# State-space loop: the adds on GpSimd set into VectorE's PSUM reads, two wide rotation passes on VectorE, output weights scaled by ScalarE

## What is computed

```
bbr = fr[..., None] * br - fi[..., None] * bi
bbi = fr[..., None] * bi + fi[..., None] * br
bu_r = jnp.einsum('blgc,gpc->blgp', uf, bbr)
bu_i = jnp.einsum('blgc,gpc->blgp', uf, bbi)
_, _, xr, xi = lax.associative_scan(_complex_affine_combine, (a_r, a_i, bu_r, bu_i), axis=1)
y = (jnp.einsum('blgp,gcp->blgc', xr, c_re) - jnp.einsum('blgp,gcp->blgc', xi, c_im)
     + d_skip * uf)
y = jax.nn.gelu(y.reshape(bsz, seq, SSM_WIDTH), approximate=False)
```

## Time and profile before

| | |
|---|---|
| median of 3 runs | 5059.5 us (5055.14 to 5059.69) |
| the profiled execution's own time | 5057.54 us |
| its span, first to last instruction | 5055.7 us |
| the loop's block, 256 to 430 us of the span | 174 us, 3.4% of the span |
| busy in that block | VectorE 160.9, TensorE 111.8, GpSimd 94.9, ScalarE 1.3 us |
| mean granted TensorE clock, whole span / in that block | 0.963 / 0.81 |

### The profile page before, as it was taken

One profiled execution on the slowest core, in us unless ns is written; L12 is line 12 of the kernel. 1 busy time (PEld: TensorE's weight loads), 2 busy tenths in 40 slices (PEclk: granted clock), 3 DMA queues, 4 the chain that ended last, 5 costly groups with the idle time before them and its releaser, 6 DMA issues. The chain is left out here.

```text
span 5055.7 us, 51526 instructions
## 1 busy us (share of the span) xinstructions
PE 4678.1 (93%) x19788; PEld 3543.7 (70%) x19788; DVE 2261.2 (45%) x4552; ACT 1444.6 (29%) x2163; POOL 1938.2 (38%) x884
## 2 busy tenths in 40 slices
PE   7667889999999999999999988899999997787999
PEld 6224757888888788888788745668878874355787
DVE  8697346983333233333440253454234136654440
ACT  3302322334444211111322234332222232233321
POOL 3054414446666444444444400334444431012443
PEclk9788989999999999999999989999999999998999
DMA  3011313445545656555222200212222221011222
GB/s 113 25 29 46 111 34 102 132 137 178 175 163 179 200 187 191 184 188 181 88 96 96 96 23 14 84 63 94 93 92 96 95 86 40 17 53 54 90 96 84
DMA packets 213172, 519.23 MB, mean 103 GB/s; under 512 B 16960, under 2 KB 82752, under 8 KB 210112
## 3 DMA queue, kind: packets, MB, share of 16 engines
q1 hardware_dynamic: 128448, 448.82, 27.0%
q10 hardware_dynamic: 84480, 67.12, 4.2%
HBM read 446.66 MB, written 69.21 MB: 102 GB/s over the span
## 5 line engine op out<-in xcount | busy, mean ns | idle before, releaser
L187 POOL TENSOR_TENSOR ring_rounded<-ring,highs_rounded 128x1024 fp32r<-128x1024 f32 x687 | 1683.7, 2452 | 2767.2 <-ACT highs_rounded L181 2767.2
L395 PE MATMUL bank<-arena_rounded,ring_rounded 128*128 128x512 f32 (+1 forms) x4488 | 1790.9, 399 | 99.6 <-DVE hT_rounded L413 41.4
L397 PE MATMUL bank<-arena_rounded,highs_rounded 128*128 128x512 f32 (+1 forms) x4488 | 1776.9, 396 | 0.0
L181 ACT ACTIVATE highs_rounded<-ring 128x1024 fp32r<-128x1024 f32 x687 | 727.9, 1061 | 2107.3 <-PE bank L397 1605.5
L396 PE MATMUL bank<-hT_rounded,highs_rounded 128*128 128x512 f32 x3128 | 1228.5, 393 | 0.0
L395 PEld LDWEIGHTS bank<-arena_rounded,ring_rounded 128*128 128x128 f32 x4488 | 854.0, 190 | 293.4 <-issue 86.1
L397 PEld LDWEIGHTS bank<-arena_rounded,highs_rounded 128*128 128x128 f32 x4488 | 852.6, 190 | 205.1
L396 PE MATMUL bank<-arena_rounded,highs_rounded 128*128 128x512 f32 (+1 forms) x2112 | 821.5, 389 | 0.0
L396 PEld LDWEIGHTS bank<-hT_rounded,highs_rounded 128*128 128x128 f32 x3128 | 593.3, 190 | 141.4
L396 PEld LDWEIGHTS bank<-arena_rounded,highs_rounded 128*128 128x128 f32 x2112 | 402.1, 190 | 86.9
L1248 DVE TENSOR_TENSOR arena<-qT,arena 128x512 f32<-128x512 f32 x64 | 150.6, 2354 | 372.2 <-ACT qT L1213 371.6
(11 more groups left out here) (325 smaller groups left out, 4684.9 us busy)
## 6 DMA issues: line engine op xcount, KB each, us to landing
ring<-pages_in SPq DMA_DIRECT2D x687, 512.0 KB, 3.4
act_table<-arena SPq DMA_DIRECT2D x128, 256.0 KB, 4.0
gate_table<-qT SPq DMA_DIRECT2D x16, 2048.0 KB, 7.3
arena<-act_table ACTq DMA_DIRECT2D x128, 256.0 KB, 4.0
arena<-gate_table ACTq DMA_DIRECT2D x32, 1024.0 KB, 8.4
arena<-ssm_in SPq DMA_DIRECT2D x16, 256.0 KB, 2.6
arena<-mem_in SPq DMA_DIRECT2D x3, 1024.0 KB, 4.8
xT<-x_in SPq DMA_DIRECT2D x8, 256.0 KB, 6.4
```

The lines of the kernel that those rows point to most:

```text
L181: nc.scalar.activation(f32r(page_high(p)), slot(p), ACT.Copy).then_inc(masked_pages.sem, 1)
L187: nc.gpsimd.tensor_tensor(f32r(slot(p)), slot(p), part_of(page_high(p)), ALU.subtract).then_inc(split_pages.sem, 1)
L395: low_last = nc.tensor.matmul(out, f32r(w_low), f32r(x_high), start=start, stop=False)
L397: return low_last, nc.tensor.matmul(out, f32r(w_high), f32r(x_high), start=False, stop=stop)
```

## The change

All of it is in `ssm`. For each tile:

- The fourth product of the turn carries a factor -1 (br * -1 * s), so that GpSimd's two instructions are both adds. `shifted` is signalled twice, after the second and after the fourth product. The first add waits for the first signal. The second add of tile t also waits for `weighed`, until VectorE is through with scan(t-1).
- The four products that turn the result forward are two instructions of 128x1024 on VectorE: both scanned halves, which now lie side by side, times cs into `by_cos`, and then times sn in place. GpSimd has no products any more.
- The output weights are made by ScalarE: four scaled copies of 128x128 (`scaled_c`), then one add of 128x256 on VectorE ahead of the scans, then a negated copy by ScalarE. They have three blocks for each tile in place of two.
- TensorE's matmuls are the same in number and shape; outputs(t) waits for `paired` and for the second `weighed`. SyncE's transfer for tile t waits for `made` and `scored` of tile t-4 and no longer for `mixed`.

The diff, with unchanged lines between left out:

```diff
     bct = [arena[:, 14592 + 512 * b:15104 + 512 * b].rearrange("p (m s) -> p m s", m=4) for b in range(depth + 1)]
-    cf = [arena[:, 16640 + 256 * b:16896 + 256 * b].rearrange("p (m s) -> p m s", m=2) for b in range(depth)]
+    cf = [arena[:, 16640 + 384 * b:17024 + 384 * b].rearrange("p (m s) -> p m s", m=3) for b in range(depth)]
+    scaled_c = arena[:, 17792:18304].rearrange("p (m s) -> p m s", m=4)
     tmp = [qT[:, 8 + j, :] for j in range(8)]
-    def part(t, j):
-        i = 4 * (t % depth) + j
-        return arena[:, 10496 + 512 * i:11008 + 512 * i] if i < 8 else hT[:, i - 4, :]
+    def halves(t, j):
+        if t % depth < 2:
+            at = 10496 + 2048 * (t % depth) + 1024 * j
+            return arena[:, at:at + 1024].rearrange("p (h n) -> p h n", h=2)
+        return hT[:, 4 + 2 * j:6 + 2 * j, :]
...
-                    sp.wait_ge(mixed.sem, mixed.at(t - depth))
+                    sp.wait_ge(made.sem, made.at(t - depth))
+                    sp.wait_ge(scored.sem, scored.at(t - depth))
                 sp.dma_start(bct[t % (depth + 1)], ssm_dram[t]).then_inc(drawn.sem, 16)
...
-                    pe.wait_ge(shifted.sem, shifted.at(t - 1))
+                    pe.wait_ge(shifted.sem, shifted.at(2 * (t - 1)))
                 for half in range(2):
...
-                pe.wait_ge(weighed.sem, weighed.at(t + 1))
-                pe.wait_ge(copied.sem, copied.at(t + 1))
-                for at, (c, j) in enumerate(((0, 0), (0, 2), (1, 1), (1, 3))):
-                    last = nc.tensor.matmul(bank[4 + t // 4][:], cf[t % depth][:, c, :], part(t, j),
+                pe.wait_ge(paired.sem, paired.at(t + 1))
+                pe.wait_ge(weighed.sem, weighed.at(2 * t + 2))
+                by_cos, by_sin = halves(t, 0), halves(t, 1)
+                for at, (c, moving) in enumerate(((0, by_cos[:, 0, :]), (2, by_sin[:, 1, :]),
+                                                  (1, by_sin[:, 0, :]), (1, by_cos[:, 1, :]))):
+                    last = nc.tensor.matmul(bank[4 + t // 4][:], cf[t % depth][:, c, :], moving,
                                             start=(t % 4 == 0 and at == 0), stop=(t % 4 == 3 and at == 3))
...
         def _(pool):
-            for t in range(n + 1):
-                if t < n:
-                    pool.wait_ge(shifted.sem, shifted.at(t + 1))
-                    nc.gpsimd.tensor_tensor(part(t, 0), part(t, 0), part(t, 1), ALU.add)
-                    nc.gpsimd.tensor_tensor(part(t, 2), part(t, 2), part(t, 3),
-                                            ALU.subtract).then_inc(summed.sem, 1)
-                if t >= 1:
-                    pool.wait_ge(exped.sem, exped.at(t))
-                    nc.gpsimd.tensor_tensor(part(t - 1, 0), part(t - 1, 1), cs[:, t - 1, :], ALU.mult)
-                    nc.gpsimd.tensor_tensor(part(t - 1, 1), part(t - 1, 1), sn(t - 1),
-                                            ALU.mult).then_inc(copied.sem, 1)
+            for t in range(n):
+                for h in range(2):
+                    pool.wait_ge(shifted.sem, shifted.at(2 * t + h + 1))
+                    if h == 1 and t >= 1:
+                        pool.wait_ge(weighed.sem, weighed.at(2 * t))
+                    nc.gpsimd.tensor_tensor(halves(t, 0)[:, h, :], halves(t, 0)[:, h, :], halves(t, 1)[:, h, :],
+                                            ALU.add).then_inc(summed.sem, 1)
...
                 br, bi = bank[2 * (t % 2)][:], bank[2 * (t % 2) + 1][:]
+                by_cos, by_sin = halves(t, 0), halves(t, 1)
                 if t >= depth:
...
                 dve.wait_ge(scored.sem, scored.at(t + 1))
-                nc.vector.tensor_tensor(part(t, 0), br, c, ALU.mult)
-                nc.vector.tensor_tensor(part(t, 1), bi, s, ALU.mult)
-                nc.vector.tensor_tensor(part(t, 2), bi, c, ALU.mult)
-                nc.vector.tensor_tensor(part(t, 3), br, s, ALU.mult).then_inc(shifted.sem, 1)
-                cr, ci = bct[t % (depth + 1)][:, 2, :], bct[t % (depth + 1)][:, 3, :]
-                cr2, ci2 = cf[t % depth][:, 0, :], cf[t % depth][:, 1, :]
-                dve.wait_ge(drawn.sem, drawn.at(16 * (t + 1)))
-                nc.vector.tensor_scalar(cr2, cr, fr[:, t:t + 1], None, ALU.mult)
-                link(nc.vector.tensor_scalar(ci2, cr, nfi[:, t:t + 1], None, ALU.mult))
-                nc.vector.scalar_tensor_tensor(out=cr2, in0=ci, scalar=nfi[:, t:t + 1], in1=cr2,
-                                               op0=ALU.mult, op1=ALU.add)
-                nc.vector.scalar_tensor_tensor(out=ci2, in0=ci, scalar=nfr[:, t:t + 1], in1=ci2,
-                                               op0=ALU.mult, op1=ALU.add)
+                nc.vector.tensor_tensor(by_cos[:, 0, :], br, c, ALU.mult)
+                nc.vector.tensor_tensor(by_sin[:, 0, :], bi, s, ALU.mult).then_inc(shifted.sem, 1)
+                nc.vector.tensor_tensor(by_cos[:, 1, :], bi, c, ALU.mult)
+                nc.vector.scalar_tensor_tensor(out=by_sin[:, 1, :], in0=br, scalar=-1.0, in1=s, op0=ALU.mult,
+                                               op1=ALU.mult).then_inc(shifted.sem, 1)
...
                 r = mag[:, t:t + 1].broadcast_to([P, SEQ])
-                dve.wait_ge(summed.sem, summed.at(t + 1))
-                nc.vector.tensor_tensor_scan(part(t, 1), r, part(t, 0), 0.0, ALU.mult, ALU.add)
-                nc.vector.tensor_tensor_scan(part(t, 3), r, part(t, 2), 0.0, ALU.mult,
+                by_cos, by_sin = halves(t, 0), halves(t, 1)
+                dve.wait_ge(copied.sem, copied.at(t + 1))
+                nc.vector.tensor_tensor(cf[t % depth][:, 0:2, :], scaled_c[:, 0:2, :], scaled_c[:, 2:4, :],
+                                        ALU.add).then_inc(made.sem, 1)
+                dve.wait_ge(summed.sem, summed.at(2 * t + 2))
+                nc.vector.tensor_tensor_scan(by_sin[:, 0, :], r, by_cos[:, 0, :], 0.0, ALU.mult, ALU.add)
+                nc.vector.tensor_tensor_scan(by_sin[:, 1, :], r, by_cos[:, 1, :], 0.0, ALU.mult,
                                              ALU.add).then_inc(exped.sem, 1)
                 dve.wait_ge(exped.sem, exped.at(t + 1))
-                nc.vector.scalar_tensor_tensor(out=part(t, 2), in0=part(t, 3), scalar=-1.0,
-                                               in1=sn(t), op0=ALU.mult, op1=ALU.mult)
-                nc.vector.tensor_tensor(part(t, 3), part(t, 3), cs[:, t, :],
+                nc.vector.tensor_tensor(by_cos, by_sin, cs[:, t, :][:, None, :].broadcast_to([P, 2, SEQ]),
+                                        ALU.mult).then_inc(weighed.sem, 1)
+                dve.wait_ge(weighed.sem, weighed.at(2 * t + 1))
+                nc.vector.tensor_tensor(by_sin, by_sin, sn(t)[:, None, :].broadcast_to([P, 2, SEQ]),
                                         ALU.mult).then_inc(weighed.sem, 1)
...
         def _(act):
+            for t in range(n):
+                cr, ci = bct[t % (depth + 1)][:, 2, :], bct[t % (depth + 1)][:, 3, :]
+                act.wait_ge(drawn.sem, drawn.at(16 * (t + 1)))
+                if t >= 1:
+                    act.wait_ge(made.sem, made.at(t))
+                for m, (part, by) in enumerate(((cr, fr), (cr, nfi), (ci, nfi), (ci, nfr))):
+                    last = nc.scalar.activation(scaled_c[:, m, :], part, ACT.Identity, scale=by[:, t:t + 1])
+                last.then_inc(copied.sem, 1)
+                act.wait_ge(made.sem, made.at(t + 1))
+                nc.scalar.activation(cf[t % depth][:, 2, :], cf[t % depth][:, 0, :], ACT.Copy,
+                                     scale=-1.0).then_inc(paired.sem, 1)
             for c in range(4):
...
     drawn.close(16 * n)
-    for s in (scored, shifted, summed, exped, copied, weighed, mixed):
+    for s in (scored, exped, copied, made, paired, mixed):
         s.close(n)
+    for s in (shifted, summed, weighed):
+        s.close(2 * n)
     turned.close(4)
```

## The result

The changed kernel took 5019.45 us (median of 4 runs, 5015.94 to 5025.98), the kernel before 5059.59 in the same comparison. The ratio is 0.9924, with a 95% interval of 0.9906 to 0.9941: 40 us or 0.8% faster. The forecast was 5020.7. The profiled execution of the changed kernel is its slowest run, 5025.98 us with a span of 5024.2, so the loop is compared by its own length and not by the span. Of the 36.6 us that the loop gained between the two profiled executions, 31.5 arrived in the span: the stages before the loop took 2.4 us longer (265.64 in place of 263.20) and those behind it 2.7 (4628.6 in place of 4625.9), with the same instructions.

A forecast was written before the change was run, and what follows sets the result against it. VectorE, partly held by GpSimd, was taken to bound the loop. The periods' 36.2 us + 2.4 at the start - 0.6 for a slow pass + 0.8 at the end = 38.8, so 5059.5 - 38.8 = 5020.7 us; range 5013 to 5031.

The forecast's parts named there:

- The bound, and the hold: In the loop VectorE sets the pace, 10.01 us a pass; GpSimd's work holds its SBUF instructions, not its PSUM reads.
- Rival (b): In the turn, GpSimd's adds hold VectorE's PSUM reads after all: pass again 10.0 us, time about 5057; chance 0.04.
- The pass, 7.60: VectorE's new loop pass: 2.40 + 0.44 + 1.13 + 1.23 + 1.26 + 1.14 = 7.60 us, against 10.01.
- the prediction's choice of the row over the rule: The held 128x256 add ends 0.28 us after GpSimd; beginning anew at GpSimd's end would be 0.14 later, 2 us in sum.
- ScalarE at no cost: ScalarE's four scaled copies and the negated one, 2.0 us of a 7.6 us pass, cost nothing.
- The one slow pass that I had foreseen: Outputs(0), after a long idle time, runs at the low clock and ends at 282.0, turn(3) due 281.4: 0.6 us lost once.
- rival (a): TensorE's clock falls again and again in the loop: 0.6 us a pass, +8.4 us if all 14 are slow, 5029; chance 0.12.
- Rival (c): TensorE's clock stays at 1.2 GHz through the loop and sets the pace: 49 us together, 5070; chance 0.02.
- The prediction's words against it: Against a low clock throughout: after seven slow records it rose in each pass before, and TensorE would be busy without a gap.
- The ends: Start of the loop 2.4 us saved; from scan(15)'s start to the loop's end 10.2 in place of 11.01, 0.8 saved.
- The sum: Whole loop: 36.2 + 2.4 - 0.6 + 0.8 = 38.8 us gained, passed on whole to the kernel's time.
- a change of length behind the loop: Stages behind the loop depend only on its end; the forecast is wrong if they change their own length.

The follow-up runs named there:

- after_again: The changed kernel run once more as it is, in a later comparison: 5022.36 us (median of 5), ratio to the kernel before 0.9927.
- dve_weights: The changed kernel with the output weights made by VectorE's four small instructions again, in place of ScalarE's four copies and the add: 5026.91 us, ratio to before 0.9937.
- warm: The changed kernel with TensorE's two input matmuls of each tile from the fourth on done twice: 5011.0 us, one run, beside 5048.4 for the kernel before.
- b_act_weights: The kernel before with only the output weights changed, to ScalarE's four scaled copies and one VectorE add: 5046.3 us, one run, beside 5048.4 for the kernel before.
- narrow: The changed kernel with the two 128x1024 products as four of 128x512, without the wait between: 5029.6 us, one run.
- no_self_wait: The changed kernel without VectorE's wait on its own first wide product: 5016.3 us, one run, beside 5048.4 for the kernel before.

## Why the prediction was right

**The bound, and the hold.** Right, and shown from both sides: placing the adds alone brings 0.86 us a pass, leaving the placing out of the change costs 1.0, and PSUM reads weren't held in any of the traces (0.67 to 0.69 us each). Rival (b) is out.

**The pass, 7.60.** Measured 7.69 in the steady passes. The step that is off is GpSimd's start. I put it 0.08 us behind the last product, from L1353 and L1328 in the earlier trace rows, and it is 0.14 (370.02 to 370.16); with the starts 1.23 apart and 1.27 for an add, GpSimd ends 2.72 behind the turn's start in place of 2.64. Everything behind that was as worked out: the add of 128x256 ends 0.28 after GpSimd, and the rest is 1.13 + 1.23 + 1.26 + 1.14. The passes of 7.60 are those in which GpSimd had been let go earlier than VectorE, which had waited for TensorE, or had no add of a tile before it.

The Trainium skill says of the shared ports (SBUF — State Buffer, section "SBUF: two separate sides") that whoever starts first has them for the whole instruction and the other is blocked fully, and it limits this on VectorE's side to instructions with two SBUF inputs or in a mode that uses both ports. The traces agree on this: the turn's products, with one SBUF input, weren't held, and held scans ended 1.07 to 1.09 us after GpSimd in six kernels. They also show, beyond, that a held instruction ends sooner after the release than it would take alone (0.28 against 0.42 for 256 elements, 1.08 against 1.21 for the scan), so that the prediction's choice of the row over the rule was right by 0.14 us a pass.

**ScalarE at no cost.** Right. Its copies end at 374.5 where VectorE needs them at 380.0. The gelu table's load lies beside the last scan.

**TensorE.** The one slow pass that I had foreseen came (8.16, 0.5 over the usual 7.69; I had 0.6). A second came unforeseen (8.80, 1.1 over), a little of rival (a), which at 0.6 in every pass was far too much; in after_again, the same kernel, only the foreseen one came (8.10). The gap's length, by which I had weighed it, doesn't decide alone, as the two outputs behind gaps of 2.30 and 2.31 show. What the Trainium skill says for this case (TensorE: Matmul & The Clock Gate, section "A second HAM failure mode: psum-queue depth-cycling") is told there of one bfloat16 kernel: it goes round PSUM banks, idles shortly between groups of matmuls, and its clock swings. The traces of this float32 loop agree in kind: outputs of 3.67, 5.37 and 6.75 us, and 3.6 to 3.67 once the gaps were filled. In this kernel the swing hides behind VectorE nearly always. In dve_weights, with longer gaps, it shows in every second pass up to 337.4. Rival (c), the low clock throughout, never came near. The prediction's words against it, that the clock rose after seven slow records in each pass before, don't fit every pass: from 320 to 405 us the outputs before took 5.06 to 5.37 us, so it rose sooner there.

**The ends.** Start: turn(1) 2.66 behind turn(0), where I took 3.0 from a range of 2.4 to 3.4. End: 10.29, where I had 10.2.

**The sum.** 38.8 foretold for the loop, 36.6 measured: 0.3 more at the start, 0.1 less at the end, and 2.4 less between: about 1.1 for GpSimd's later start (twelve passes of 0.09), 1.0 for TensorE (1.6 where I had 0.6), 0.3 for GpSimd's one late start. That the median lies within 1.3 us of the forecast is partly luck: the stages outside the loop, with the same instructions, moved by several us between runs (4625.9 us from the skip term to the end before, 4628.6 after, 4626.1 in after_again, 4620.0 in warm). The prediction passed the loop's whole gain on and named a change of length behind the loop as a sign of being wrong. The stages there did change by 2.7 us and those ahead by 2.4, and the profiled execution took 5025.98 where 5018.7 was foretold. That they change by as much between executions of the changed kernels speaks for noise and against an effect of the change.

**Where the gain comes from.** By the pass, the two parts that I tried alone bring the kernel before 0.86 (placing) and 0.54 (ScalarE weights) of 10.01. Taken out of the change, placing loses 1.0, ScalarE weights 0.65 and the products 0.7 to 0.85, together about 2.4, where the change gained 2.32. So the parts nearly add up, and the losses of the loop do too (34.3 us against the execution with 129.97, which gained 36.6). That isn't because each removes its own work. ScalarE's weights took 2.65 us of VectorE's stretch away in the kernel before and brought 0.54, since the hold went over to the scans; taken out of the change they cost about as much because the four small instructions are nearly free of holds there. Moving the products alone to VectorE in the kernel before wasn't tried.

## What to carry to other kernels

Where GpSimd works beside VectorE on SBUF, read a held instruction's duration against that of the same shape elsewhere: what looks like VectorE's work may be waiting, and taking the work away then only moves the wait to the next instruction. Put GpSimd's work over VectorE's PSUM reads (worth 0.86 to 1.0 us of a pass here), count when it can start (what releases it, and the queue in front of it), and give it a stretch as long as its work. And check whether a wait between two instructions of the same engine guards anything: here it ate all that the doubled width had gained.

## What the runs showed of the hardware that was not expected

- Released by a wait on two semaphores, GpSimd started 0.14 us after VectorE's last product and TensorE 0.15; released by one, GpSimd started 0.08 after. That the second semaphore is the cause was not tested.
- Holds take turns. With GpSimd's adds against two scans (b_act_weights) neither engine ran twice in a row: adds of 1.38 and 2.18 us, scans of 2.28 and 2.22.
- GpSimd started late at the same place in the loop in the changed kernel (twice), in warm and in narrow (a pass of 8.03 to 8.05 each time, and 7.91 in place of 7.57 in no_self_wait), for a reason that the trace doesn't show. It stays open.
